# Differential attention: the two sub-heads of a head walk the key tiles together

## What is computed

```python
def attend(q, k, v, scale):          # per head: softmax(scale * q k^T) v
    ...
    s = jnp.einsum('bqhgd,bkhd->bhgqk', qblk, kf)
    p = jax.nn.softmax(s, axis=-1)
    return jnp.einsum('bhgqk,bkhd->bqhgd', p, vf)

def diff_attention(q, k, v, p, lam_init):
    ...
    o1 = attend(q[..., 0, :], k[..., 0, :], v, scale)   # sub-head 0, 32 wide
    o2 = attend(q[..., 1, :], k[..., 1, :], v, scale)   # sub-head 1, 32 wide, the same v
    o = rmsnorm(o1 - lam * o2, p['diff_subln_g']) * (1.0 - lam_init)
```

## Time and profile before

| | |
|---|---|
| time, median of 2 runs | 4175.25 us (4170.26 and 4180.24) |
| the profiled execution's own time | 4151.62 us |
| its span on the slowest core (core 7) | 4150.6 us |
| spans of all cores | 4124.3 to 4150.6 us |
| mean granted TensorE clock, core 7 | 0.704 |
| busy: PE, PEld, DVE, ACT, POOL | 68%, 38%, 37%, 40%, 12% |

### The profile page before, as it was taken

How to read it: one execution, slowest core, us unless ns; L and a number is a source line. 1 busy time by engine, 2 the same in 40 slices (tenths; PEclk the granted TensorE clock), 3 DMA queues, 4 the chain that set the end, 5 groups by cost and what they waited for, 6 DMA issues and landing times.

```text
span 4150.6 us, 58892 instructions; the slowest of 8 cores (4124.3 to 4150.6 us)
## 1 busy us (share of the span) xinstructions
PE 2811.0 (68%) x16898; PEld 1576.8 (38%) x16898; DVE 1549.6 (37%) x4493; ACT 1662.3 (40%) x3356; POOL 486.7 (12%) x728
## 2 busy tenths in 40 slices
PE   1342343675689667469925688986994678987796
PEld 0331332332238433223812233443482223443365
DVE  5945933444422444442234411224223531223322
ACT  2301203663420466242023476674303367675310
POOL 3432430011010001101000000110101000010100
PEclk8555556755799875579957755577996755567898
DMA  6546543112463211255350000125533000011742
GB/s 102 65 62 94 67 70 64 48 32 58 48 78 47 57 46 35 53 64 67 42 133 5 6 12 6 34 46 70 70 42 52 1 11 1 20 37 38 92 57 67
DMA packets 363136, 207.17 MB, mean 50 GB/s; under 512 B 138850, under 2 KB 342882, under 8 KB 362820
## 3 DMA queue, kind: packets, MB, share of 16 engines
q0 software_dynamic: 174720, 120.20, 21.7%
q1 hardware_dynamic: 188100, 83.20, 9.3%
HBM read 290.45 MB, written 33.10 MB: 78 GB/s over the span
## 4 chain that ended last, share of the span: by engine, by line
PE 55%; DMA 15%; issue 9%; ACT 9%; DVE 8%; POOL 2%; SPq 1%; DVEq 0%; ACTq 0%; POOLq 0%
PE ps L395 45%; PE ps L1124 6%; DMA arena<-mlp_w 4%; PE ps L407 3%; ACT L376 2%; POOL arena L356 2%; DVE arena L356 2%; DMA ssm_scr_b<-arena 2%; ACT pT L376 2%; DMA arena<-ssm_d 1%; PE ps L400 1%; DMA arena<-cdv 1%; DMA arena<-w_ada 1%; DVE tokf L356 1%; ACT tokb L382 1%
## 5 line engine op out<-in xcount | busy, mean ns | idle before, releaser
L395 PE MATMUL ps<-arena 128*128 128x256 bf16 (+7 forms) x5376 | 1051.0, 329 | 179.9 <-DVE arena L356 118.9
L376 ACT ACTIVATE pT<-ps 128x512 bf16<-128x512 f32 (+1 forms) x1280 | 700.8, 555 | 690.0 <-PE ps L395 625.5
L395 PEld LDWEIGHTS ps<-arena 128*128 128x128 bf16 (+4 forms) x5376 | 565.0, 110 | 318.7 <-issue 210.2
L395 PE MATMUL ps<-actT,arena 128*128 128x512 bf16 x2048 | 473.8, 394 | 106.0 <-DMA arena<-mlp_w 89.0
L1124 PE MATMUL ps<-arena,pT 128*128 128x65 bf16 x3584 | 362.4, 235 | 115.2 <-ACT pT L376 90.5
L395 PE MATMUL ps<-arena,actT 128*128 128x512 bf16 (+1 forms) x1536 | 384.9, 405 | 66.5 <-DVE stat L430 22.9
L356 POOL TENSOR_TENSOR arena<-arena 128x128 f32<-128x128 f32 (+1 forms) x320 | 299.0, 934 | 967.6 <-DVE arena L356 751.5
L1124 PEld LDWEIGHTS ps<-arena,pT 128*128 128x128 bf16 x3584 | 240.4, 119 | 416.9 <-issue 405.3
L395 PEld LDWEIGHTS ps<-actT,arena 128*128 128x128 bf16 x2048 | 202.3, 101 | 373.1 <-issue 158.8
L376 ACT ACT_TABLE_LOAD x211 | 270.7, 1283 | 117.5 <-DMA arena<-ssm_log_dt 40.6
L356 DVE TENSOR_TENSOR arena<-arena 128x128 f32<-128x128 f32 (+6 forms) x384 | 245.8, 649 | 46.7 <-POOL arena L356 20.9
(11 more groups left out here) (166 smaller groups left out, 2826.6 us busy)
## 6 DMA issues: line engine op xcount, KB each, us to landing
arena<-mlp_w POOLq DMA_DIRECT2D x64, 512.0 KB, 6.1
arena<-mlp_w POOLq DMA_DIRECT2D x16, 2048.0 KB, 22.4
arena<-w_ada POOLq DMA_DIRECT2D x24, 1024.0 KB, 14.5
arena<-ssm_scr_b SPq DMA_DIRECT2D x256, 64.0 KB, 2.2
arena<-ssm_scr_f SPq DMA_DIRECT2D x128, 128.0 KB, 2.5
arena<-w_in POOLq DMA_DIRECT2D x4, 3776.0 KB, 25.6
ssm_scr_f<-arena SPq DMA_DIRECT2D x16, 512.0 KB, 10.9
ssm_scr_b<-arena SPq DMA_DIRECT2D x32, 256.0 KB, 6.6
```

The costliest lines, as they stand in the source:

```text
L376: return E("act", lambda h: h.activation(out=out, in_=in_, func=func, **kw), reads, writes, cost=ecost("act", fsz(out)) + (0.1 if accum_ou ...
L395: ins = h.matmul(out, lhsT=l, rhs=r, start=(i == 0), stop=(i == n - 1))
```

## The change

For a differential head the two sub-heads become one group with a common loop over the key tiles. For every key tile one PE operation does both QK matmuls (sub-head 0 from partitions 0 to 31 into one score bank, sub-head 1 from partitions 32 to 63 into the other), and it signals once, behind the second. Then come exp and PV of sub-head 0, and exp and PV of sub-head 1. Both output banks are held by the group. Both epilogues come behind the last key tile; their small statistics tiles (`st`) get separate columns. GQA and MLA items become groups of one and keep their operations, banks and costs. The QK operation of a pair is given the cost 0.1 + 1.2 x (0.035 + qb/2400), which for S is 0.398, where a single one has 0.348.

```diff
-            items = []
+            groups = []
             for h_ in range(4):
                 for qi_ in range(nqb):
-                    for j_ in range(2):
-                        items.append((2 * h_ + j_, qi_))
+                    groups.append(([spec(2 * h_), spec(2 * h_ + 1)], qi_))
...
-                    for kk in range(nk):
-                        kt = kt0 + kk
-                        bs = att_s_rot.next()
-                        mm(psf(bs)[:, 0:qb], [(KT[r0:r1, kh, kt * 128:(kt + 1) * 128], QT[r0:r1, qh, q0:q0 + qb])],
-                           [(kkey, kt)] + [(qkey, t_) for t_ in qtiles], [pk(bs)])
+                bos = [att_o_rot.next() for _ in specs]
...
+                for kk in range(nk):
+                    kt = kt0 + kk
+                    bss = [att_s_rot.next() for _ in specs]
+
+                    def qk(hh, bss=bss, kt=kt, specs=specs, q0=q0):
+                        ins = None
+                        for sp, bs in zip(specs, bss):
+                            ins = hh.matmul(psf(bs)[:, 0:qb], lhsT=sp["KT"][sp["r0"]:sp["r1"], sp["kh"], kt * 128:(kt + 1) * 128],
+                                            rhs=sp["QT"][sp["r0"]:sp["r1"], sp["qh"], q0:q0 + qb], start=True, stop=True)
+                        return ins
+                    E("pe", qk, [(specs[0]["kkey"], kt)] + [(specs[0]["qkey"], t_) for t_ in qtiles], [pk(bs) for bs in bss],
+                      cost=0.1 + (0.035 + qb / 2400.0) * (1.0 if len(specs) == 1 else 1.2))
+                    for sp, bs, bo, ops_ in zip(specs, bss, bos, opss):
                         pi = pT_rot.next()
-                        actf(pT[pi][:, 0:qb], psf(bs)[:, 0:qb], AF.Exp, [pk(bs)], [("pT", pi)], scale=scale)
+                        actf(pT[pi][:, 0:qb], psf(bs)[:, 0:qb], AF.Exp, [pk(bs)], [("pT", pi)], scale=sp["scale"])
...
+                        E("pe", pv, [("pT", pi), (sp["vkey"], kt)], [pk(bo)], cost=0.1 + nsub * 0.09)
+                for sp, bo, ops_ in zip(specs, bos, opss):
+                    kind, h, j = sp["kind"], sp["h"], sp["j"]
+                    sc_ = 48 + 4 * j if kind == "d" else 48
```

More of the change, by code:

```diff
@@ L1080, in attention, with spec @@
         att_o_rot = Rot([2, 3])
+        def spec(hs):
+            if hs < 8:
+                h, j = hs // 2, hs % 2
+                return dict(kind="d", h=h, j=j, QT=dqT, KT=dkT, V=dV, vh=h, r0=32 * j, r1=32 * j + 32, scale=32 ** -0.5,
+                            qh=h, kh=h, qkey="dqT", kkey="dkT", vkey="dV")
+            if hs < 12:
+                h = hs - 8
+                return dict(kind="g", h=h, j=0, QT=gqT, KT=gkT, V=gV, vh=h // 2, r0=0, r1=64, scale=64 ** -0.5,
+                            qh=h, kh=h // 2, qkey="gqT", kkey="gkT", vkey="gV")
+            h = hs - 12
+            return dict(kind="m", h=h, j=0, QT=mqT, KT=mkT, V=mV, vh=h, r0=0, r1=96, scale=96 ** -0.5,
+                        qh=h, kh=h, qkey="mqT", kkey="mkT", vkey="mV")
         for sq in range(nseq):
@@ new lines, in attention @@
+                    groups.append(([spec(hs_)], qi_))
+            for (specs, qi) in groups:
+                q0 = tile0 * 128 + qi * qb
+                qtiles = [tile0 + qi * nsub + s_ for s_ in range(nsub)]
+                mk_ = [("mixed", t_) for t_ in qtiles]
+                bos = [att_o_rot.next() for _ in specs]
+                opss = [psf(bo)[:, 0:nsub * 65].rearrange("p (s d) -> p s d", s=nsub) for bo in bos]
+                for kk in range(nk):
[10 more added lines that the diff above has]
+                    for sp, bs, bo, ops_ in zip(specs, bss, bos, opss):
@@ L1118, in attention, with pv @@
                         pi = pT_rot.next()
-                        actf(pT[pi][:, 0:qb], psf(bs)[:, 0:qb], AF.Exp, [pk(bs)], [("pT", pi)], scale=scale)
-                        def pv(hh, pi=pi, kt=kt, kk=kk, ops_=ops_, V=V, vh=vh):
+                        actf(pT[pi][:, 0:qb], psf(bs)[:, 0:qb], AF.Exp, [pk(bs)], [("pT", pi)], scale=sp["scale"])
+                        def pv(hh, pi=pi, kt=kt, kk=kk, ops_=ops_, V=sp["V"], vh=sp["vh"]):
                             ins = None
@@ L1126, in pv @@
                             return ins
[L1127 to L1130, removed]
+                        E("pe", pv, [("pT", pi), (sp["vkey"], kt)], [pk(bo)], cost=0.1 + nsub * 0.09)
+                for sp, bo, ops_ in zip(specs, bos, opss):
+                    kind, h, j = sp["kind"], sp["h"], sp["j"]
+                    sc_ = 48 + 4 * j if kind == "d" else 48
+                    E("dve", lambda h_, ops_=ops_, sc_=sc_: h_.reciprocal(st_(sc_, sc_ + nsub), ops_[:, :, 64]), [pk(bo)], [("st", sc_)])
+                    rec = st_(sc_, sc_ + nsub).unsqueeze(2).to_broadcast([128, nsub, 64])
                     if kind == "d":
                         dst = o1 if j == 0 else o2
-                        tt("dve", dst[:, 0:nsub, :], ops_[:, :, 0:64], rec, ALU.mult, [pk(bo), ("st", 48)], [("tokf", j)])
+                        tt("dve", dst[:, 0:nsub, :], ops_[:, :, 0:64], rec, ALU.mult, [pk(bo), ("st", sc_)], [("tokf", j)])
                         if j == 1:
@@ L1139, in attention @@
                             tt("pool", sqv, dif, dif, ALU.mult, [("tokf", 2)], ["tmpf"])
[L1140 to L1144, removed]
+                            E("dve", lambda h_, sqv=sqv: h_.tensor_reduce(out=st_(56, 56 + nsub), in_=sqv, axis=AX.X, op=ALU.add),
+                              ["tmpf"], [("st", 56)])
+                            rstd_chain(st_(56, 56 + nsub), st_(44, 44 + nsub), 1.0 / 64, ("st", 56), ("st", 44))
+                            tt("dve", dif, dif, st_(44, 44 + nsub).unsqueeze(2).to_broadcast([128, nsub, 64]), ALU.mult,
+                               [("tokf", 2), ("st", 44)], [("tokf", 2)])
                             mdst = mixed[:, qtiles[0]:qtiles[0] + nsub, h * 64:(h + 1) * 64]
@@ L1150, in attention @@
                         mdst = mixed[:, qtiles[0]:qtiles[0] + nsub, c0:c0 + 64]
-                        tt("dve", mdst, ops_[:, :, 0:64], rec, ALU.mult, [pk(bo), ("st", 48)], mk_)
+                        tt("dve", mdst, ops_[:, :, 0:64], rec, ALU.mult, [pk(bo), ("st", sc_)], mk_)
     def ssm_run(job, l):
```

## The result

The changed kernel takes 4244.9 us (median of 9 runs) against 4165.2 us (7 runs) of the kernel before, 80 us more: a ratio of 1.019, 95% interval 1.0162 to 1.0217. It is slower, by about 2%; 4260 us was forecast, from 4175 us. Times, ratios and intervals here leave out the executions in which one die's cores show a lower granted clock and the time is some per cent longer (here 2 of 11 after, at 4275 and 4355 us, and 3 of 10 before). Ratios are to runs of the kernel before that were taken beside each kernel; their medians are 4162 to 4167 us.

What follows compares the result with a forecast made beforehand. In S's differential heads PE was taken as tightest, with ACT and handoffs close behind. +79 us in S and +6 in P gave +85 on a 4175 us median, 4260 us; range 4190 to 4345 us.

Steps and rivals of the forecast that it cites:

- The ring: Differential heads in S: QK and exp no longer overlap, so a pair's key-tile turn is 2.29 us against 1.80.
- PV ahead of QK: PE's order in S: sub-head 1's PV (0.34 us) goes before the next pair's QK, by 0.062 or a tie.
- Rival 2: In S, QK stands ahead of sub-head 1's PV: turn 1.95 us, 4200 us in all; chance 0.14.
- the prediction's own formula for PV's path: Scheduler's model in S: PV leads to the next exp with 0.46 + 0.25 + bl(exp 1).
- Side by side: A pair's two QK matmuls stream at once, the second costing 0 of a possible 0.446 us a turn.
- rival 1: The two QKs queue instead: turn 2.74 us, a pair 34.0 us, 4342 us in all; chance 0.25.
- The pair: One pair of sub-heads in S takes 29.1 us against 24.14, +4.95 us.
- The square root: In S, its 2.82 us partly fill ACT's 1.21 us gap and lengthen one turn per pair by 1.61 us.
- The sum over S: 8 pairs in each of 2 layers of S, 16 x 4.95 = +79 us.
- P: Job P: attention grows 24 us but the SSM ends the stage, so +6 us, bounds 0 and +24.
- rival 3: The longer attention in P is all on the path: +79 + 24, 4278 us; chance 0.06.
- rival 4: Faster: granted clock rises in the differential stages, turn 1.90 us, still no gain in S; faster or anything else, 0.05.

Runs made afterwards that it cites:

- experiment 2: Changed kernel with each QK of a pair as its own operation with its own wait and signal; two executions, 4170.0 and 4188.4 us, no ratio.
- experiment 4: Changed kernel with four score banks and four pT tiles for the pairs in S; 4056.4 us, ratio 0.9724.
- 5: Changed kernel with four score banks in S but still two pT tiles; 4094.6 us, ratio 0.9828.
- experiment 6: Changed kernel with four pT tiles in S but still two score banks; 4191.0 us, ratio 1.0065.
- 7: Changed kernel with four pT tiles and two score banks in S, PE's order put back to PV, PV, QK by a dependency; 4242.0 us, ratio 1.0202.
- experiment 1: Changed kernel with the guessed cost of the pair's QK 0.2 higher, so QK goes ahead of the second PV; 4189.9 us, ratio 1.005.
- experiment 3: Changed kernel with sub-head 1 reading the same 32 partitions as sub-head 0; 4334.6 us, ratio 1.0391.
- experiment 9: Kernel before with pairs in P only, 4175.5 us, ratio 1.0031; second kernel, four banks and four pT in S, single sub-heads in P, 4063.4 us.

## Why the prediction was right, point by point

- **The ring.** The forecast's turn of 2.29 us, from 0.76 + 1.08 + 0.11 + 0.34, was 2.28 as 0.71 + 1.09 + 0.11 + 0.35. That it is the common wait and signal with two score banks was shown from both sides: separate signals bring S back to its old length (experiment 2), a second pair of banks breaks the ring (4, 5), more pT doesn't (6, 7). No run takes the common wait and the common signal apart.
- **PV ahead of QK.** As forecast, and decisive: experiments 1 and 7 move 50 to 55 us with nothing but this order. Rival 2 had 4200 us, 0.6% above before; experiment 1 measured a ratio of 1.005. That the order hangs on the pT edge stood in the prediction's own formula for PV's path, yet I didn't draw on it when I wrote the expectation of experiment 6.
- **Side by side.** The two QKs took 0.60 us together, against 1.03 on the same rows (3). The nearest row, the two matmuls 0.21 us apart at the earlier trace rows, was a row of the same-rows case. By the Trainium skill, "TensorE: Matmul & The Clock Gate", Part 3 (packing small matmuls), matmuls on different 32-row groups run at the same time; the trace agrees, with 0.60 for two where one takes 0.60, and starts 0.003 us apart (2460.136 and 2460.139). (Where the prediction says behind this page that otherwise "the second rival holds", it is its rival 1 that would.)
- **The pair.** 29.1 us was forecast, 29.08 measured. The square root cost what was worked out: one turn around it is 2476.34 to 2480.26, 3.92 us in the trace of the changed kernel, 1.64 longer than the rest; the forecast was 1.61.
- **The sum over S was too high: +79 forecast, +63 measured.** The term was mis-sized by taking 8 pairs a layer. The first pair overlaps the end of the input projection, which sets its length: from the first QK to the first exp table are 39.9 us after (2408.25 to 2448.13) and 42.9 before (2358.18 to 2401.07). Seven pairs count, 7 x 4.94 = 34.6, less 3.0 there: 31.6, measured 31.8 and 31.2.
- **P.** +6 forecast, +4 measured in the stages, +3 in experiment 9; the P stages also grew by 2 to 3 us each in the two kernels with single sub-heads there, so no run shows that this is the pairing's. That the SSM ends the stage and covers the rest fits these +1 to +3 us a layer, and they speak against rival 3, which had +24 in all; the time of experiment 9, -2 to +27 us, can't exclude it.
- **The clock** stayed at 0.50 in the differential stages in the changed kernel and in experiment 4, where PE was busy 83%. So rival 4 didn't come up. Its "a third twice" is the cut in P that would be needed with S still at +79 us; with its own full clock, a pair in S at about 24.6 us, a sixth would do.
- **The total.** +85 us on 4175 was forecast, +80 on 4165 measured. S came out 16 us under its term, and some 10 us that no term had and that lie in none of the stages filled most of that. That the total is closer than its parts is luck; the turn, the pair and the order are not.

## What to carry to other kernels

Joining two operations into one signal also joins their waits: with only as many buffers as the joined operation fills, the two engines take turns, however much work runs side by side inside it. So give the group a second set of buffers in the same edit, here two idle PSUM banks, and the same pairing that costs 2% gains 2.8%. And where a list scheduler breaks near ties between the consumer of one buffer and the producer of the next, read the emitted order: an unrelated buffer count can flip it, and the flip can look like the buffer's own worth.

## What the runs showed of the hardware

- Two 32-row, 512-column matmuls on different partitions and different banks took 0.60 us together, at the 0.50 clock, and 1.03 us on the same partitions (experiment 3).
- Exps queued in a row start 0.48 to 0.49 us apart though each shows 0.60 us (two in 1.08 us, four in 2.06 us). So ACT's "idle before" of 0.2 to 0.4 us in the earlier trace rows understates its room, and a busy share that is added up from such records overstates its load: 93.8 of 99 us in experiment 4, where PE sets the turn.
